# The scan's turns: TensorE's transposing form for the lower head, products with the identity for the upper

## The reference, cut to what matters

```
def _wkv7_step(S, inp):
    r_t, w_t, k_t, v_t, aa_t, bb_t = inp
    sa = jnp.einsum('zbhij,zbhj->zbhi', S, aa_t)
    S = S * w_t[..., None, :] + sa[..., :, None] * bb_t[..., None, :] + v_t[..., :, None] * k_t[..., None, :]
    y = jnp.einsum('zbhij,zbhj->zbhi', S, r_t)
    return S, y
...
    seq = tuple(jnp.moveaxis(_flip_bwd(z), 2, 0) for z in (r2, w_h, k_h, v2, aa, bb))
    S0 = jnp.zeros((2, b, N_HEADS, HEAD_DIM, HEAD_DIM), f32)
    _, ys = lax.scan(_wkv7_step, S0, seq)
```

## Time and profile before

| | |
|---|---|
| time, median of 3 runs | 4773.38 us (4772.42 to 4777.04) |
| the profiled execution | 4783.78 us, of which the span 4781.5 us |
| TensorE's clock over the span | 0.946 of full speed |
| busy, of the span | TensorE products 89%, weight loads 75%, VectorE 41%, ScalarE 29%, GpSimd 27% |
| the scan | about 2540 to 3500 us |
| the turns in it | L1589 and L1592, 3840 of 49032 products |

### The profile page before, as it was taken

How to read it: one execution, slowest core, us unless ns; L and a number is a source line. 1 busy time by engine, 2 the same in 40 slices (tenths; PEclk the granted TensorE clock), 3 DMA queues, 4 the chain that set the end, 5 groups by cost and what they waited for, 6 DMA issues and landing times. The chain is left out here.

```text
span 4781.5 us, 110964 instructions
## 1 busy us (share of the span) xinstructions
PE 4249.0 (89%) x49032; PEld 3572.1 (75%) x49032; DVE 1967.8 (41%) x3539; ACT 1366.6 (29%) x2860; POOL 1287.7 (27%) x874
## 2 busy tenths in 40 slices
PE   3899988999999998897967888888878999999997
PEld 2688956888888887675756777777755888888885
DVE  3011055244143351326217777777733254252441
ACT  1111166211011111236314555555532211111110
POOL 1211033311111113311106555555512311111110
PEclk6899989999999999898979999999989999999998
DMA  4212242411312213121232222222132312313214
GB/s 133 59 55 65 70 122 85 127 32 40 128 36 80 84 35 114 51 80 45 78 100 70 69 70 76 75 76 73 52 127 79 113 36 62 102 40 102 62 53 161
DMA packets 402635, 372.29 MB, mean 78 GB/s; under 512 B 63057, under 2 KB 370513, under 8 KB 399985
## 3 DMA queue, kind: packets, MB, share of 16 engines
q1 hardware_dynamic: 390320, 354.75, 24.1%
q10 hardware_dynamic: 11840, 10.49, 0.6%
HBM read 257.68 MB, written 107.48 MB: 76 GB/s over the span
## 5 line engine op out<-in xcount | busy, mean ns | idle before, releaser
L422 POOL TENSOR_TENSOR f_wlow<-f_raw,f_whigh 128x1024 fp32r<-128x1024 f32 (+1 forms) x152 | 360.2, 2370 | 1670.8 <-ACT f_whigh L493 1670.8
L478 PE MATMUL f_ps<-fx_hh,f_whigh 128*128 128x512 f32 (+1 forms) x2112 | 530.2, 359 | 0.0
L478 PE MATMUL f_ps<-fx_hl,f_whigh 128*128 128x512 f32 (+1 forms) x2112 | 528.9, 358 | 0.0
L478 PE MATMUL f_ps<-fx_hh,f_wlow 128*128 128x512 f32 (+1 forms) x2112 | 528.5, 358 | 0.0
L493 ACT ACTIVATE f_whigh<-f_raw 128x1024 fp32r<-128x1024 f32 (+1 forms) x152 | 156.5, 1030 | 923.0 <-PE f_ps L478 895.5
L478 PEld LDWEIGHTS f_ps<-fx_hh,f_whigh 128*128 128x128 f32 x2112 | 349.4, 189 | 65.1
L478 PEld LDWEIGHTS f_ps<-fx_hl,f_whigh 128*128 128x128 f32 x2112 | 349.2, 189 | 65.4
L478 PEld LDWEIGHTS f_ps<-fx_hh,f_wlow 128*128 128x128 f32 x2112 | 348.9, 189 | 65.1
L478 PE MATMUL f_ps<-mo_oh,f_whigh 128*128 128x512 f32 (+1 forms) x1440 | 360.5, 359 | 25.5 <-POOL f_wlow L422 25.5
L478 PE MATMUL f_ps<-mo_ol,f_whigh 128*128 128x512 f32 (+1 forms) x1440 | 359.8, 358 | 0.0
L478 PE MATMUL f_ps<-mo_oh,f_wlow 128*128 128x512 f32 (+1 forms) x1440 | 359.6, 358 | 0.0
(11 more groups left out here) (267 smaller groups left out, 8399.5 us busy)
## 6 DMA issues: line engine op xcount, KB each, us to landing
f_xo<-xres SPq DMA_DIRECT2D x64, 640.0 KB, 4.0
xres<-f_xo SPq DMA_DIRECT2D x56, 640.0 KB, 2.9
f_raw<-in_ffn_w_gate SPq DMA_DIRECT2D x44, 512.0 KB
f_raw<-in_ffn_w_up SPq DMA_DIRECT2D x44, 512.0 KB
sc_rk<-rkvl SPq DMA_DIRECT2D x80, 256.0 KB, 3.3
rkvl<-ri_ot SPq DMA_DIRECT2D x28, 640.0 KB
f_raw<-in_ffn_w_down SPq DMA_DIRECT2D x32, 448.0 KB
qkv_raw<-in_na_w_qkv SPq DMA_DIRECT2D x24, 512.0 KB, 5.5
```

The source lines that it names most:

```text
L422: nc.gpsimd.tensor_tensor(wlow[:, m % 2, 0:kt], raw[:, 0:kt], whigh[:, m % 2, 0:kt].bitcast(F32), ALU.subtract).then_inc(cut_lo, 1)
L478: last = nc.tensor.matmul(ps[:, m % 2, n, 0:count], w[:, m % 2, k], x[:, k, t0:t0 + count], start=(k == 0 and w is whigh and x is xh), sto ...
```

## The change

In turn(), nc.tensor.matmul with the identity becomes nc.tensor.transpose for the lower head's three arrays of each unit, with the same array, the same block of the identity and the same place in PSUM. The upper head's stay as they were. The order of the instructions, the waits and the semaphore at the end are the same; lower and upper still alternate.

```
+                low_half, high_half = halves
+
                 def turn(G, z, half):
...
                     for s in (2 * half, 2 * half + 1):
                         u = unit(z, s)
                         for a in range(2):
-                            for rows in halves:
-                                nc.tensor.matmul(turn_ps[z][rows, 0, a * W + s * C:a * W + (s + 1) * C], rec[rows, r, z, u, a], ident[rows, rows],
-                                                 start=True, stop=True)
-                        for rows in halves:
-                            last = nc.tensor.matmul(turn_ps[z][rows, 1, s * C:(s + 1) * C], vb[rows, r, z, u * C:(u + 1) * C], ident[rows, rows],
-                                                    start=True, stop=True)
+                            at = slice(a * W + s * C, a * W + (s + 1) * C)
+                            nc.tensor.transpose(turn_ps[z][low_half, 0, at], rec[low_half, r, z, u, a], ident[low_half, low_half])
+                            nc.tensor.matmul(turn_ps[z][high_half, 0, at], rec[high_half, r, z, u, a], ident[high_half, high_half],
+                                             start=True, stop=True)
+                        at, of = slice(s * C, (s + 1) * C), slice(u * C, (u + 1) * C)
+                        nc.tensor.transpose(turn_ps[z][low_half, 1, at], vb[low_half, r, z, of], ident[low_half, low_half])
+                        last = nc.tensor.matmul(turn_ps[z][high_half, 1, at], vb[high_half, r, z, of], ident[high_half, high_half],
+                                                start=True, stop=True)
                     if half:
                         last.then_inc(pe_turn[z], 1)
```

## The result

The changed kernel takes 5174.59 us (5169.21 to 5183.06) against 4772.9: 402 us more, ratio 1.0842, interval 1.0829 to 1.0856. The forecast was 4755, its range ended at 4872. The cheaper half of rival (D) was inside it, the dearer half, 4961, was not, and even that falls 214 us short.

The account below looks back on a forecast made before the run. The prediction took the scan as bound for much of its time by how fast TensorE's instructions arrive. Fewer instructions gave -18 us, form changes 0: from the 4773.4 us median to 4755, range 4738 to 4872.

Parts of the forecast that it names:

- rival (D): Scan's turns: array empties at every change between transpose and product; +99 or +188 us, 4872 or 4961; chance 0.24.
- Part (1): Lower head's turns: transposes leave one record instead of two, so 960 products and 960 weight loads go, 1920 instructions.
- Part (2): Array time in turn(): a transpose takes 55 to 60 ns; call stays at 0.70 us, array gain zero.
- Part (5): Possible added cost at each of 12 form changes a call: between 0 and 0.09 us, taken as 0.
- Rival (E): TensorE's clock falls in the turns, their 112 us at worst taking twice as long; 4885 us; chance 0.03.
- (C): Scan's turns: transpose and product do not run together although their quarters differ; +10 us, 4783; chance 0.13.
- Part (3): Scan: 1920 fewer instructions, 7.5 packets, shorten TensorE's waits for instructions; 18 us gained, between 4 and 31.
- Part (4): Waits and queues unchanged; VectorE's L1912 ahead of L1568 costed at nothing, at most all 18 us lost.

Follow-up runs that it names:

- t2_low_first: Changed kernel with all six transposes of a turn() call ahead of its six upper products, 2 changes of form a call; 4792.32 us, ratio 1.0041.
- b_low: Kernel before the change, with the lower head's turns as bf16 products of each number's upper 16 bits, no transposes; 4762.75 us, ratio 0.9988.
- p0_low_first: Kernel before the change, products only, all six of the lower head ahead of the upper head's six in each call; 4788.36 us, ratio 1.0031.

## Why the prediction was wrong, point by point

- **Part (1), the count**: right, 960 products and 960 weight loads fewer; the instruction queue brings 380 packets in place of 387 over the whole program.
- **Part (2), the array time of one transpose**: right, 55 ns. Its conclusion, that the lower quarter works beside the upper and a call stays at 0.70 us, is the step that failed: the call takes 2.4 us.
- **Part (5), the change of form**: the term behind that step, taken at 0 from a row in which products of two lines followed each other without a gap. That row holds products only and says nothing of the form. The upper bound, 0.09 us a change, was about right for each (0.145 to 0.17 instead of 0.055; 0.15 back instead of 0.058); I had the price and put it on the wrong side of the choice. The earlier trace rows had the nearer row: L901's last transpose starts at 702.22 + 0.87 - 0.27 = 702.82 and L913 at 703.03, 0.21 us instead of 0.12. They differ in shape as well as in form, so the row alone would not have decided.
- **Rival (D)** named the mechanism and the place. Its price at full clock, 0.244 us a pair, lacked the third part: behind a change the two records of a product stand 0.11 us apart instead of 0.058. With it a pair costs 0.43 - 0.116 = 0.31 us more, 300 us in all. The stalls absorbed more than the 46 us that I allowed: over the scan they fell by 61 us.
- **Rival (E)**, the clock, was kept apart from (D) with 0.03. It came with (D): where the form changes 12 times a call, the granted clock falls to half in nearly every group. By the estimate above about 190 us are (D)'s, next to its dearer price of 188; that is luck, since the pair and what would be absorbed were both priced too low. About 210 are the clock's, nearly twice the 112 of (E), because the turns had become longer and other products run at the lower level too. Together they make the 402 us; apart, neither reaches it. The row against it, clock 1.00 around L901, is of a stretch whose transposes follow each other in runs of 4 or 6. The Trainium skill says that the full clock does not engage for transposing (TensorE: Matmul & The Clock Gate, Part 4); this isn't borne out here as a statement on transposes: t2_low_first has the same 960 of them and a clock of 0.98. With the same transposes the order makes the difference, 0.98 in runs of six and 0.80 in turns; what in the turns brings the clock down, the holes or the forms, no run here separates.
- **The Trainium skill's Restrictions** (TensorEngine Tiling (Array Packing)), which speak against an FP32 transpose under column tiling, were given as a reason for (C) or (D), and I set nothing against them but the zero of part (5). The trace shows that the lower quarter's transpose runs, at 55 ns, but not beside products.
- **Part (3)**, the gain by fewer instructions: b_low bears the mechanism out, with 24 us less of stalls; the size was 6 to 9 us and not 18. **Part (4)** had costed the wait for L1912 at nothing; in b_low it took 10 us more, so the truth lay between nothing and its bound of all 18. In the changed kernel itself neither can be told from the rest.

## What to carry to other kernels

Transposes in TensorE's own form and fp32 products did not run beside each other here: group them, so that the form changes once in many instructions, or leave a small turn as a product with the identity, which runs beside others. What the form would give with both heads' turns in it was not run. When a step may open many holes in TensorE's work, price the clock with it; here it doubled the loss. Where the stalls of an engine are spread evenly over all lines and come every 256 instructions or so, the engine waits for its own program: there extra array time was partly free, and less of it, or fewer instructions, gave little before the next engine's wait took over.

## What the runs showed of the hardware that was not expected

- Two forms do not follow each other closely even within one quarter, although each alone runs at 55 to 58 ns a record: 0.17 us from transpose to product, 0.15 back at full clock, against none for a change between bf16 and fp32.
- TensorE's clock fell to half in stretches in which the busy time said 100%: 13.00 of 13.00 us busy with 135 products.
- Array time can be added for a fraction of its length: in p0_low_first some 80 us of it cost 16.
